# The second block's mixer: stick heads as running products against differences of values, stick values projected last, keys in rooms of their own

## The reference

```python
q  = rms_norm(cq, q_a_norm) @ w_q_up        # 8 heads of 96
kv = rms_norm(ckv, kv_a_norm) @ w_kv_up     # 8 heads: 64 of key, 64 of value
q, k = rope_tail(rms_norm(q)), rope_tail(rms_norm([k_nope, k_rope]))
mla  = causal_softmax_attention(q, k, v)
# stick heads, for a query i and keys j < i:
z = (sq @ sk.T) * 64 ** -0.5
log_beta, log_1m_beta = log_sigmoid(z), log_sigmoid(-z)          # the latter 0 where j >= i
suffix = reversed_cumsum(log_1m_beta) - log_1m_beta
a = where(j < i, exp(log_beta + suffix), 0)
sb = a @ sv
out = concat([mla, sb]) @ w_o
```

## Time and profile before

| what | us |
|---|---|
| median of 3 runs (2158.17 to 2161.47) | 2158.98 |
| the profiled execution, its time | 2163.58 |
| the profiled execution, its span | 2161.7 |
| TensorE idle before the last transposes of `in2`, from the timeline | 11.69 |
| `mix` (scores of step 0 to the first product of out2) | 994.2 to 1090.2 |

### The profile page before, as it was taken

The page is one execution under the profiler, slowest core; times in us unless marked ns, Lnnn a source line. Parts: engine busy times, 40 slices in busy tenths (PEclk is TensorE's granted clock), DMA queues, the critical chain, the costliest instruction groups (busy, mean ns, idle before and its releaser), DMA issues.

```text
span 2161.7 us, 29403 instructions
## 1 busy us (share of the span) xinstructions
PE 1979.8 (92%) x10416; PEld 1604.6 (74%) x10416; DVE 829.9 (38%) x1453; ACT 501.9 (23%) x1253; POOL 1116.5 (52%) x731
## 2 busy tenths in 40 slices
PE   5777899789999998987799999999999899999999
PEld 4666566578888887874478888887787578888887
DVE  4763667554535105545723222102453623212100
ACT  2111466322222102225511010101132511101100
POOL 4434001157666663622746666666553446666663
PEclk9887899699999998999899999999999999999999
DMA  4212000123333231312013333332321113333332
GB/s 135 59 57 88 0 0 4 37 88 98 97 97 115 89 102 56 89 34 69 11 50 98 97 97 96 94 95 76 83 85 59 41 40 92 97 96 95 97 97 88
DMA packets 125373, 161.99 MB, mean 75 GB/s; under 512 B 11670, under 2 KB 87398, under 8 KB 125286
## 3 DMA queue, kind: packets, MB, share of 16 engines
q1 hardware_dynamic: 121440, 159.97, 24.2%
q10 hardware_dynamic: 3846, 0.82, 0.2%
HBM read 158.66 MB, written 2.10 MB: 74 GB/s over the span
## 4 chain that ended last, share of the span: by engine, by line
PE 82%; DVE 9%; ACT 3%; issue 2%; POOL 2%; DMA 1%; ACTq 0%; SPq 0%; DVEq 0%; POOLq 0%
PE ps L718 22%; PE ps L720 22%; PE ps L719 22%; PE ps L1156 3%; PE ps L1085 2%; PE ps L1177 2%; PE ps L733 2%; PE ps L851 1%; PE ps L1168 1%; DVE tok L1827 1%; PE ps L1274 1%; PE ps L1126 1%; PE ps L1061 1%; DVE xt_lo L1837 1%; ACT dump L1395 1%
## 5 line engine op out<-in xcount | busy, mean ns | idle before, releaser
L447 POOL TENSOR_TENSOR w_lo<-raw,w_hi 128x1024 fp32r<-128x1024 f32 (+1 forms) x256 | 614.7, 2401 | 21.4
L445 POOL TENSOR_SCALAR w_hi<-raw 128x1024 fp32r<-128x1024 f32 (+1 forms) x256 | 275.4, 1076 | 574.0 <-PE ps L720 497.3
L718 PE MATMUL ps<-xt_hi,w_hi 128*128 128x512 f32 (+1 forms) x1160 | 432.9, 373 | 7.2 <-DVE xt_lo L1837 6.5
L720 PE MATMUL ps<-xt_hi,w_lo 128*128 128x512 f32 (+1 forms) x1160 | 432.2, 373 | 0.0
L719 PE MATMUL ps<-xt_lo,w_hi 128*128 128x512 f32 (+1 forms) x1160 | 432.2, 373 | 0.0
L718 PE MATMUL ps<-w_hi,xt_hi 128*128 128x512 f32 (+3 forms) x672 | 264.1, 393 | 28.7 <-ACT tok L1666 20.0
L720 PE MATMUL ps<-w_hi,xt_lo 128*128 128x512 f32 (+3 forms) x672 | 259.1, 386 | 0.0
L719 PE MATMUL ps<-w_lo,xt_hi 128*128 128x512 f32 (+3 forms) x672 | 258.9, 385 | 0.0
L718 PEld LDWEIGHTS ps<-xt_hi,w_hi 128*128 128x128 f32 x1160 | 219.2, 189 | 47.0 <-DVE xt_lo L1837 7.6
L720 PEld LDWEIGHTS ps<-xt_hi,w_lo 128*128 128x128 f32 x1160 | 219.0, 189 | 38.7
L719 PEld LDWEIGHTS ps<-xt_lo,w_hi 128*128 128x128 f32 x1160 | 219.2, 189 | 38.3
(11 more groups left out here) (317 smaller groups left out, 2480.3 us busy)
## 6 DMA issues: line engine op xcount, KB each, us to landing
raw<-in_w_up SPq DMA_DIRECT2D x88, 256.0 KB
raw<-in_l_w_gate SPq DMA_DIRECT2D x88, 256.0 KB
raw<-in_l_w_up SPq DMA_DIRECT2D x88, 256.0 KB
raw<-in_l_w_down SPq DMA_DIRECT2D x40, 512.0 KB
raw<-in_l_w_in SPq DMA_DIRECT2D x36, 512.0 KB
raw<-in_w_down SPq DMA_DIRECT2D x20, 512.0 KB
raw<-in_l_w_o SPq DMA_DIRECT2D x16, 512.0 KB
raw<-in_w_in SPq DMA_DIRECT2D x12, 512.0 KB
```

Source lines behind the costliest of these rows:

```text
L445: e.tensor_scalar(w_hi[:, s, 0:width], r, 1.0, 0.0, ALU.mult, ALU.add).then_inc(split, 1)
L447: e.tensor_tensor(w_lo[:, s, 0:width], r, w_hi[:, s, 0:width].bitcast(F32), ALU.subtract).then_inc(split, 1)
L718: e.matmul(o, s_hi, m_hi, start=start, stop=False)
L720: return e.matmul(o, s_lo, m_hi, start=False, stop=stop)
```

## The change

The stick heads' sum is rearranged: the sum over j of (R(j+1) - R(j)) v(j) equals the sum of (1 - R(j)) (v(j) - v(j-1)), with v(-1) = 0. So the scan is done in place, the difference of neighbours on GpSimd goes, and the copies of turned stick steps give 1 - R. The stick values are differenced once: after the projection ScalarE issues two DMAs that copy them one token down into `v_back`, GpSimd waits for these and subtracts in place, and only then goes on to `pool_pairs`. In `in2` K1 comes before SV, and SV is last; K0 and K1 are staged in rooms of their own, `km_b` lies in the room of the gains, and SP loads the gains only after the last soft scores.

```diff
     IN2 = [(416, 0, 4, 2), (512, 4, 4, 2), (384, 8, 1, 2), (512, 9, 4, 2), (384, 13, 1, 2), (512, 14, 1, 1),
-           (512, 15, 4, 2), (512, 19, 1, 1)]
-    CQ, SQ, Q0, SK, Q1, K0, SV, K1 = range(8)
+           (512, 15, 1, 1), (512, 16, 4, 2)]
+    CQ, SQ, Q0, SK, Q1, K0, K1, SV = range(8)
...
+    km_b = gains[0:MQK, :, :].rearrange("p a (k n) -> p (a k) n", n=SEQ)
...
-        gain_load(e, 6, at("in2_tp", 27))
+        sp_group(e, ph["out2"].g0, two_kt(A["l0_w_o_2"], 0, W))
+        gain_load(e, 6, at("mix_s", 16))
         gain_load(e, 7)
-        with e.Fori(0, 2) as c:
-            sp_group(e, c + ph["out2"].g0, two_kt(A["l0_w_o_2"], c * W, W))
+        sp_group(e, ph["out2"].g0 + 1, two_kt(A["l0_w_o_2"], W, W))
...
-        def sticks(g):
-            for x in range(2):
-                u = 2 * (g - 4 * st.soft) + x + 1
-                e.wait_ge(*at(f"{name}_sc", u))
-                r = run_at(g, x)
-                n = (4 - g % 4) * P
-                e.tensor_tensor(prob_at(g, x), r[:, 1:n + 1], r[:, 0:n], ALU.subtract).then_inc(sem(f"{name}_w"), 1)
...
+        e.wait_ge(*at("in2_copy", 32))
+        e.memset(v_back[0:1, 0, :], 0.0).then_inc(sem("v_first"), 1)
+        e.wait_ge(*at("v_first", 1))
+        e.wait_ge(*at("v_back", 32))
+        for t in range(NT):
+            e.tensor_tensor(v2[:, t, W:D], v2[:, t, W:D], v_back[:, t, :], ALU.subtract).then_inc(sem("v_step"), 1)
         pool_pairs(e, mix, {3 + 4 * s: (ph["out2"].g0, s) for s in range(4)})
...
-        return tok_b if name == "in2" and c == K0 else tok3
+        return tok_k[c - K0] if name == "in2" and c in (K0, K1) else tok3
...
             else:
-                e.wait_ge(*at(f"{name}_w", 2 * (g - 4 * st.soft) + 2))
+                e.wait_ge(*at(f"{name}_sc", 2 * (g - 4 * st.soft) + 2))
...
+            if p == st.soft:
+                e.wait_ge(*at("v_step", NT))
...
-                   {(SQ, 2): (CQ,), (Q0, 0): (SQ,), (SK, 2): (Q0,), (Q1, 0): (SK,), (SV, 1): (Q1,), (SV, 3): (K0,)},
+                   {(SQ, 2): (CQ,), (Q0, 0): (SQ,), (SK, 2): (Q0,), (Q1, 0): (SK,), (SV, 1): (Q1,), (SV, 2): (K0,), (SV, 3): (K1,)},
...
+                    if st.is_soft(g):
+                        op = e.activation(turned_probs(st, g, y), turned_bank(g, y), ACT.Copy)
+                    else:
+                        op = e.activation(turned_probs(st, g, y), turned_bank(g, y), ACT.Identity, scale=-1.0, bias=1.0)
...
-            act_copies(e, od, "in2", c, ends[c], copy2(c), plan, c not in (K0, SV))
+            act_copies(e, od, "in2", c, ends[c], copy2(c), plan, c not in (K0, K1, SV))
             if c == CQ or c in HEAD_CHUNKS:
                 act_rstd(e, od, "in2", 1 if c == CQ else HEAD_CHUNKS[c] + 2, 8 if c == CQ else 16)
-            for x in {Q1: (), K0: (Q1, K0), SV: ()}.get(c, (c,)):
+            for x in {Q1: (), K0: (), K1: (Q1, K0), SV: (K1,)}.get(c, (c,)):
                 act_turned(e, od, "in2", plan, x)
+        e.wait_ge(*at("in2_copy", 32))
+        e.dma_start(v_back[1:P, :, :], v2[0:P - 1, :, W:D]).then_inc(sem("v_back"), 16)
+        e.dma_start(v_back[0:1, 1:NT, :], v2[P - 1:P, 0:NT - 1, W:D]).then_inc(sem("v_back"), 16)
         act_pair_attend(e, od, mix)
...
-                if h >= 4:
-                    e.wait_ge(*at(f"{name}_w", 2 * (h - 4) + x + 1))
-                e.tensor_tensor_scan(run_at(g, x)[:, 0:n][:, ::-1], prob_at(g, x)[:, ::-1],
-                                     one[:, 0:1].broadcast_to([P, n]), 1.0, ALU.mult, ALU.mult).then_inc(
+                keep = prob_at(g, x)[:, ::-1]
+                e.tensor_tensor_scan(keep, keep, one[:, 0:1].broadcast_to([P, n]), 1.0, ALU.mult, ALU.mult).then_inc(
...
+                        op = e.tensor_scalar(turned_probs(st, g, y), turned_bank(g, y), -1.0, 1.0, ALU.mult, ALU.add)
...
-        for step in (CQ, SQ, (Q0,), Q0, SK, (Q1,), (K0,), Q1, K0, (K1,), K1):
+        for step in (CQ, SQ, (Q0,), Q0, SK, (Q1,), (K0,), (K1,), Q1, K0, K1):
```

More of the change, by code:

```diff
@@ L181, in build @@
     sb("under_first", [P, 4, SEQ], F32, lay)
-    km_a = sb("km_a", [MQK, 4, SEQ], F32, lay)
+    inv_t2 = sb("inv_t2", [P, 2, SEQ], F32, lay)
+    o_sb2 = sb("o_sb2", [P, 2, SEQ], F32, lay)
     sb("under_second", [P, 4, SEQ], F32, lay)
-    km_b = sb("km_b", [MQK, 4, SEQ], F32, lay)
+    v_back = sb("v_back", [P, NT, W], F32, lay)
     lay.close()
@@ L224, in build @@
     u = ExitStack()
[L225 to L231, removed]
+    qm = sb("qm", [MQK, 8, SEQ], F32, u)
     qs = sb("qs", [P, 4, SEQ], F32, u)
@@ L234, in build @@
     v2 = sb("v2", [P, NT, D], F32, u)
+    km_a = sb("km_a", [MQK, 4, SEQ], F32, u)
     o_ = ExitStack()
@@ L239, in build @@
     cq_lo = sb("cq_lo", [P, 2, SEQ], F32R, o_)
+    tok_k = [sb(f"tok_k{i}", [P, NT, 4 * MQK], F32, o_) for i in range(2)]
     o_.close()
-    mix_rooms = dict(p_turn=sb("p_turn2", [P, 2, 2, 13, P], F32, u), inv_t=sb("inv_t2", [P, 2, SEQ], F32, u),
-                     o_sb=sb("o_sb2", [P, 2, SEQ], F32, u), inv_w=sb("inv_w2", [P, 8, HD], F32, u),
-                     inv=sb("inv2", [P, 8], F32, u))
+    mix_rooms = dict(p_turn=sb("p_turn2", [P, 2, 2, 13, P], F32, u), inv_t=inv_t2, o_sb=o_sb2,
+                     inv_w=sb("inv_w2", [P, 8, HD], F32, u), inv=sb("inv2", [P, 8], F32, u))
     u.close()
@@ L283, in build @@
         "p (k s c) -> p k s c", k=2, s=CMPS)
-    tok_b = gains[:, :, :].rearrange("p a n -> p (a n)")[:, 0:NT * 4 * MQK].rearrange("p (t n) -> p t n", t=NT)
+    km_b = gains[0:MQK, :, :].rearrange("p a (k n) -> p (a k) n", n=SEQ)
     xn = tok[:, 0:2 * D].rearrange("p (s n) -> p s n", s=2)
@@ L414, in _ @@
         slabs = (two_kt(iw, 0, 416) + two_kt(iw, 416, W) + [[(0, cols(qw, 0, 384, slice(0, 2)))]] + two_kt(iw, 928, W)
-                 + [[(0, cols(qw, 384, 384, slice(0, 2)))], [(0, cols(kw, 0, W, slice(0, 1)))]]
-                 + two_kt(iw, 1440, W) + [[(0, cols(kw, W, W, slice(0, 1)))]])
+                 + [[(0, cols(qw, 384, 384, slice(0, 2)))], [(0, cols(kw, 0, W, slice(0, 1)))],
+                    [(0, cols(kw, W, W, slice(0, 1)))]] + two_kt(iw, 1440, W))
         for i in range(ph["in2"].groups):
             sp_group(e, ph["in2"].g0 + i, slabs[4 * i:4 * i + 4])
-        gain_load(e, 6, at("in2_tp", 27))
+        sp_group(e, ph["out2"].g0, two_kt(A["l0_w_o_2"], 0, W))
+        gain_load(e, 6, at("mix_s", 16))
         gain_load(e, 7)
-        with e.Fori(0, 2) as c:
-            sp_group(e, c + ph["out2"].g0, two_kt(A["l0_w_o_2"], c * W, W))
+        sp_group(e, ph["out2"].g0 + 1, two_kt(A["l0_w_o_2"], W, W))
         sp_ffn(e, ph["up2"], ph["down2"], A["l0_w_gate_2"], A["l0_w_up_2"], 0, A["l0_w_down_2"], lambda: None)
@@ L526, in build @@
     mix = Pairs("mix", 4, 8, mix_rooms)
[L528 to L533, removed]
     def pool_pairs(e, st, slabs):
@@ L570, in pool_pairs @@
                     halves(p)
-            if st.is_soft(r - 1) or r - 1 >= st.steps:
-                continue
-            sticks(r - 1)
     def stage_queries(e, ph, q_src, rows, iters, ready, before=None):
@@ L690, in build @@
         mla_heads(km_a, 0, 1),
+        mla_heads(km_b, 0, 1),
         [],
-        mla_heads(km_b, 0, 1),
     ]
@@ L1035, in output_free, with pe_pair_attend @@
         return at(f"{st.name}_x", p + 1) if p < st.soft else at(f"{st.name}_slo", p + 1 - st.soft)
-    def pe_pair_attend(e, st, score, value, start, banks):
+    def pe_pair_attend(e, st, score, value, start, banks, later=()):
         name = st.name
@@ L1092, in pe_pair_attend @@
         for r in st.rounds:
+            if r == 1:
+                for s, v in later:
+                    e.wait_ge(s, v)
             if r < st.steps:
@@ L1308, in _ @@
         heads_of = lambda v: lambda p, x, kb: v[:, kb, (2 * p + x) * HD:(2 * p + x + 1) * HD]
-        pe_pair_attend(e, mix, mix_scores, heads_of(v2), [at("in2_tpa", 12), at("in2_tpd", 15), at("in2_copy", 32)], [])
+        pe_pair_attend(e, mix, mix_scores, heads_of(v2), [at("in2_tpa", 10), at("in2_tpd", 13), at("in2_copy", 32)], [],
+                       [at("in2_tpa", 12), at("in2_tpd", 15)])
         pe_out_direct(e, "out2", [at("mix_lo", 2), at("mix_lo", 4), at("mix_slo", 2), at("mix_slo", 4)],
@@ L1605, in turned @@
                     e.wait_ge(*at(f"{name}_t", g + 1))
-                    e.activation(turned_probs(st, g, y), turned_bank(g, y), ACT.Copy).then_inc(
-                        *od.done(*is_turned(st, g, y)))
+                    if st.is_soft(g):
+                        op = e.activation(turned_probs(st, g, y), turned_bank(g, y), ACT.Copy)
+                    else:
+                        op = e.activation(turned_probs(st, g, y), turned_bank(g, y), ACT.Identity, scale=-1.0, bias=1.0)
+                    op.then_inc(*od.done(*is_turned(st, g, y)))
         def inverses(p):
@@ L1618, in high @@
             e.wait_ge(*at(f"{name}_o", p + 1))
+            if p == st.soft:
+                e.wait_ge(*at(f"{name}_lo", st.soft))
```

(6 more changed lines are left out.)

## The result

The changed kernel takes 2192.22 us (median of 4 runs, 2189.52 to 2195.69) beside 2160.02 us for the kernel before on the same chip: ratio 1.015, 95% interval 1.0133 to 1.0168. Measured again beside later experiments it took 2191.66 us, ratio 1.0143 (1.0117 to 1.0169). The forecast was 2178.7 (2169 to 2194), slower with 0.88. The time is in the range, 13.5 us above the forecast. The profiled execution has a span of 2191.7 us, 30.0 above that of before.

The account below looks back on a forecast made before the run. TensorE, busy 92% of the span, was taken as the bound, so only its idle or slow stretches could give much. Terms -8 + 34.6 + 2.5 - 9.4 = +19.7 us gave a median of 2178.7 us (2169 to 2194).

Parts of the forecast that it names:

- The copy on one engine: Stick values' copy after the projection: 127 partitions use one DMA engine, 43 us, landing at 1031.1.
- the eleven end packets: Load on 44 partitions: 11 small packets, read as one per DMA engine used, the largest number up to 16 dividing the rows.
- The wait of +34.6: Soft pairs, step 7's transposes: TensorE waits for inverses GpSimd widens only after the copy, from 1006.6 to 1041.2, +34.6 us.
- The clock, +2.5 (0 to 4): After TensorE's idle time: a set of values and the small work run at half clock, +2.5 us.
- K1 before SV, -8 (-9 to -4): In `in2`: K1's norm is hidden by two slabs of SV, so `mix` starts earlier, -8 us.
- stall for ScalarE's banks: In `in2`: TensorE starts the fourth tile of SV's first slab only at 962.5, when ScalarE has copied K1's tile 3.
- The sticks, -9.4 (-12 to -3): Stick rounds, 1030 to 1091 us: 5 us less waiting for GpSimd's differences, 4.4 from faster value products, -9.4 us.
- The sum: Whole kernel: -8 + 34.6 + 2.5 - 9.4 = +19.7 us, giving 2183.3 on the profiled execution, 2178.7 on the median.

Follow-up runs that it names:

- e1_spread: Changed kernel with the 127-partition copy of the stick values cut into copies of 112 and 15 partitions: 2148.81 us, ratio 0.9936 to the kernel before.
- e2_swap: Changed kernel with the short copy of three runs issued ahead of the 127-partition copy: 2184.84 us, ratio 1.0115 to the kernel before.
- e9_rooms: Changed kernel with the 127-partition copy issued as four, one per room of tokens, before the short one: 2189.52 us, ratio 1.0135 to the kernel before.
- e4_order: As e1_spread, but with in2's old order, SV before K1: 2153.05 us, ratio 0.996 to the kernel before.
- e6_copy_first: As e1_spread, but VectorE does a stick round's turned copies ahead of its scans: 2139.55 us, ratio 0.9899 to the kernel before.

## Why the prediction was right, and where its terms were not

The sign was right, and so was the cause, the copy on one engine; the path from it to TensorE was another. The time was 13.5 us too low on the median, 10.3 us on the profile (2161.7 + 19.7 = 2181.4 against 2191.7).

- **The copy on one engine: right.** It landed at 1030.0 (1031.1 forecast), 0.085 us a run. The row behind it was the eleven end packets. e1_spread shows that this alone decides the sign: it lies 12.5 us below its kernel before, the changed kernel 31 to 32 above.
- **The wait of +34.6: right in size, wrong in place.** The working had "some 0.5 us" for ScalarE's issue, and "a second one, of three runs, goes with it". That second issue was costed at nothing and took 33.99 us. It held ScalarE, so TensorE idled 30.35 us from step 2 on; GpSimd's late inverses were then hidden. e2_swap, in which it isn't held, has the forecast wait (33.84). That 30.35 is near 34.6 is partly luck: the stall began at 991.9 instead of 1006.6 and ended at 1022.3 instead of 1041.2, as another wait on the same copy.
- **The clock, +2.5 (0 to 4): the term that failed,** 9.7 us of the miss. I took a short set of slow transposes after an idle of 11.69 us for a measure of what 30 us of idle would cost. The slow work was 12.15 us, spread over 28 us, and 12.1 in the profile of the second measurement. It is no fixed price: behind the same stall e9_rooms paid 4.3, and behind a wait as long but later, at the transposes of step 7, e2_swap paid 1.1 (`mix` to step 16 were 35.0 us above before, the wait 33.84). Why the clock came back late in the one and soon in the others isn't settled.
- **K1 before SV, -8 (-9 to -4): in its range, but at its small end.** The profile has -7.45, of which 0.95 lie ahead of the anchor; from there it is -6.5, and -5.1 with e1_spread. e4_order, which changes the order alone, gives 4.2. The working's stall for ScalarE's banks held: TensorE started the fourth tile of SV's first slab at 962.07 (962.5 forecast), after 4.47 us of idle, and waited 4.94 before K1's fourth.
- **The sticks, -9.4 (-12 to -3): too much,** -5.9 after, -6.1 in e1_spread, -6.4 in e4_order. TensorE's waits from step 16 to out2 fell from 17.5 us to 13.3, 4.2 against the 5 counted: those for GpSimd are gone, those for ScalarE's copies rose from 3.0 to 5.2. The six value products, of which the earlier trace rows are three, 3.81, 4.33, 4.07, 2.38, 3.64 and 2.38 us before, took 4.53, 2.38, 2.37, 2.37, 4.53 and 2.38: 2.1 us less instead of 4.4. Two sets still fell on half clock. The first stands behind TensorE's wait of 3.6 us for VectorE's copy. That wait was there before the change, as long (its line stands below), and no row of the forecast shows it: I looked at the waits that the change touches and left out the one that stays. e6_copy_first takes it away, and 7.4 us of the sticks with it.
- **The sum.** The errors by row: stall -4.2, clock +9.7, sticks +3.5, `in2` +0.5 make +9.4, and 0.9 lie outside the stretch. The stall, shorter than forecast, offset a part of the clock's and the sticks' errors.

TensorE's wait for VectorE's copy at the start of the sticks, in the profile of before:

```profile
1037.30 0.28 PE L1061 MATMUL ps<-ident,tok 64*128 64x64 f32 x2 [3.63 <-DVE p_turn L2070]
```

## What to carry to other kernels

Look at the number of partitions of a copy: 127 ran on one DMA engine, and cutting it into 112 and 15 turned a loss of 1.5% into a gain of 0.6%. A copy that nobody is waiting for can still stop the engine that issues it: issue nothing behind a long copy on one engine, and put short ones first. And look at each in-order engine's list for what stands behind an operation that waits: VectorE's copies ahead of its scans took 7.4 us off the sticks in the trace, more than the whole rearranged sum did (6.4). The wait that it removes stood in the kernel before as well; the reordering alone, without the rearranged sum, wasn't run.

## What the runs showed of the hardware that was not expected

- An issue of 6 KB was held 33.99 us behind a copy of 508 runs on one DMA engine; ahead of that copy it took 0.83, and behind the same runs on many engines 1.91.
- Four copies of 127 rows each shared one engine's pace (43.8 us together): these separate copies did not go to separate engines.
- After an idle of 30.35 us TensorE's clock stayed at 1.2 GHz through 28 us of nearly full work, and again in a second profile of the same kernel; after the same idle of 30.18 us in e9_rooms it was back after some 9 us. Fillers in the idle kept it at 2.4 GHz from 1000 to 1045 us.
